# Two expert layers: the last quarter of the down-projection's columns from each token's own fetched rows

## What is computed

```
u = u_emb[expert]
a = jax.nn.gelu(jnp.einsum('thk,td->thk' ...), approximate=False)
coef = (g * a).astype(xb.dtype)
return jnp.einsum('thk,thkd->td', coef, v_emb[expert])
```

## Time and profile before

| | |
|---|---|
| median of 3 runs | 4169.73 us |
| profiled execution, span | 4171.1 us |
| TensorE, VectorE, ScalarE, GpSimd busy | 99%, 74%, 55%, 12% |
| DMA | 831 MB, 199 GB/s over the span |
| down-projection of block 1, of block 2 | 1457 to 2154 us, 3450 to 4147 us |

### The profile page before, as it was taken

How to read it: one execution, slowest core, us unless ns; L and a number is a source line. 1 busy time by engine, 2 the same in 40 slices (tenths; PEclk the granted TensorE clock), 3 DMA queues, 4 the chain that set the end, 5 groups by cost and what they waited for, 6 DMA issues and landing times.

```text
span 4171.1 us, 72720 instructions
## 1 busy us (share of the span) xinstructions
PE 4116.5 (99%) x21876; PEld 3527.9 (85%) x21876; DVE 3099.3 (74%) x5278; ACT 2278.5 (55%) x4043; POOL 516.1 (12%) x509
## 2 busy tenths in 40 slices
PE   8999999999999999999999999999999999999998
PEld 8978898888888888888889899988888888888887
DVE  6476677885999766777769978688599985566666
ACT  5446544555666655555554465455566665555554
POOL 4100010000222211111100002000022221111110
PEclk9999999999999999999999999999999999999999
...
GB/s 223 163 121 150 202 175 194 207 207 197 191 192 191 201 220 219 231 261 246 239 212 178 176 153 184 163 210 206 199 193 190 190 198 221 216 218 238 216 219 161
DMA packets 310247, 831.31 MB, mean 199 GB/s; under 512 B 29040, under 2 KB 129136, under 8 KB 306800
## 3 DMA queue, kind: packets, MB, share of 16 engines
...
...
HBM read 779.37 MB, written 50.33 MB: 199 GB/s over the span
## 4 chain that ended last, share of the span: by engine, by line
PE 94%; DVE 4%; ACT 1%; issue 1%; DMA 0%; DVEq 0%; SPq 0%; ACTq 0%
PE psum L419 11%; PE psum L417 11%; PE psum L418 11%; PE psum L485 11%; PE psum L487 11%; PE psum L486 11%; PE psum L1717 5%; PE psum L1719 5%; PE psum L1718 5%; PE psum L1909 2%; PE psum L1911 2%; PE psum L1910 2%; PE psum L408 1%; DVE sb_w_lo L2297 1%; PE psum L426 1%; PE psum L1815 1%
## 5 line engine op out<-in xcount | busy, mean ns | idle before, releaser
L2297 DVE TENSOR_TENSOR sb_w_lo<-sb_raw,sb_w_hi 128x512 fp32r<-128x512 f32 x2736 | 1887.1, 712 | 986.5 <-ACT sb_w_hi L1998 975.5
L1998 ACT CAST sb_w_hi<-sb_raw 128x512 fp32r<-128x512 f32 x2736 | 1696.9, 623 | 1581.2 <-PE psum L487 645.0
L417 PE MATMUL psum<-sb_w_hi,sb_act_hl 128*128 128x512 f32 x2048 | 811.4, 396 | 1.1 <-DVE sb_w_lo L2297 1.1
L419 PE MATMUL psum<-sb_w_lo,sb_act_hl 128*128 128x512 f32 x2048 | 801.5, 391 | 0.0
L418 PE MATMUL psum<-sb_w_hi,sb_act_hl 128*128 128x512 f32 x2048 | 798.9, 390 | 0.0
L485 PE MATMUL psum<-sb_w_hi,sb_act_hl 128*128 128x512 f32 x2048 | 797.0, 389 | 0.8 <-DVE sb_w_lo L2297 0.8
L486 PE MATMUL psum<-sb_w_lo,sb_act_hl 128*128 128x512 f32 x2048 | 796.7, 389 | 0.0
L487 PE MATMUL psum<-sb_w_hi,sb_act_hl 128*128 128x512 f32 x2048 | 796.7, 389 | 0.0
L1717 PE MATMUL psum<-sb_act_hl,sb_w_hi 128*128 128x256 f32 x1488 | 429.8, 289 | 26.9 <-DVE sb_w_lo L2297 13.8
L419 PEld LDWEIGHTS psum<-sb_w_lo,sb_act_hl 128*128 128x128 f32 x2048 | 385.0, 188 | 82.1
L485 PEld LDWEIGHTS psum<-sb_w_hi,sb_act_hl 128*128 128x128 f32 x2048 | 384.4, 188 | 81.0 <-DVE sb_w_lo L2297 1.2
...
## 6 DMA issues: line engine op xcount, KB each, us to landing
sb_raw<-in_u SPq DMA_DIRECT2D x512, 512.0 KB, 4.2
sb_raw<-in_v SPq DMA_DIRECT2D x512, 512.0 KB, 3.5
...
sb_acts_in<-acts_mid SPq DMA_DIRECT2D x256, 128.0 KB, 3.3
acts_mid<-sb_acts_out SPq DMA_DIRECT2D x126, 256.0 KB, 5.4
...
```

The source lines that it names most:

```text
L417: pe.matmul(ps, h, w_hi[:, c, :], start=k == 0, stop=False)
L419: return pe.matmul(ps, h, w_lo[:, c, :], start=False, stop=k == 15)
L1998: act.copy(w_hi[:, c, :], raw[:, 2 * par + c // 2, (c % 2) * 512:(c % 2) * 512 + 512]).then_inc(hi_ready, 1)
L2297: dve.tensor_tensor(w_lo[:, c, :], raw[:, 2 * par + c // 2, (c % 2) * 512:(c % 2) * 512 + 512], w_hi[:, c, :].bitcast(F32), ALU.subtract). ...
```

## The change

v is cut by columns. The first 1536 (DENSE) stay dense: three quarters a tile, 18 matmuls, loads of 128x1024 and 128x512, w_hi and w_lo used as a ring of four (`down_slot`). The last 512 (PICKED) come per token: GpSimd issues an indirect DMA that fetches the 2 KB pieces of a token's own 128 experts, one per partition, into picked_rows, and another that fetches its 128 activations, 4 bytes each, from acts_mid. Four tokens (t x 128 + 32j + r, j = 0 to 3) are a group ("quad"), 64 a block, four in flight (QUAD_SLOTS). VectorE (`place`) multiplies activation and gate, and writes the coefficients into column r of a zero 128x32 matrix per token (lone). TensorE (`quad`) multiplies it with the token's rows in plain fp32 into partitions 32j to 32j+31 of bank 6 + t. Two groups follow each other behind tiles 7, 11, 15 and so on to 123, 126 and 127. GpSimd's weighing moves to VectorE; GpSimd starts with the row fetches of four groups, then their activations, then group by group as quad_used rises. VectorE makes the indices ahead of tile 0 (`make_indices`). The tiles of TensorE and VectorE in these stages are written out instead of looped, the buffers of the fetched rows lie over act_hl and scratch, and some semaphores are merged.

The core of the diff:

```diff
+PICKED = 512
+DENSE = D - PICKED
+QUADS, QUAD_SLOTS = 64, 4
...
+def quad_tile(q):
+    return min(7 + 4 * (q // 2), 96 + q // 2, 127)
+QUADS_AFTER = [[q for q in range(QUADS) if quad_tile(q) == i] for i in range(128)]
...
+        picked = nc.alloc_sbuf_tensor_at("sb_picked", [P, 14, 512], F32, offset=act_at + 2 * 512 * 4).ap()
+        picked_rows = [picked[:, n, :] for n in range(14)]
+        picked_rows += [scratch[:, lo:lo + 2, :].rearrange("p a b -> p (a b)") for lo in (4, 6)]
+        lone = scratch[:, 0:2, :].rearrange("p a b -> p (a b)").rearrange("p (n j m) -> p n j m", n=QUAD_SLOTS, j=4)
+        picked_acts, one_of, picked_coef = scratch[:, 2, :], scratch[:, 3, 0:63], scratch[:, 3, 64:80].rearrange("p (n j) -> p n j", j=4)
+        v_index, act_index = slots[:, 1, :].bitcast(U32), slots[:, 2, :].bitcast(U32)
+        by_quad = lambda v: v.rearrange("p (t j r) -> p t r j", t=QT, j=4)
...
+        def down_slot(k, c):
+            return (3 * k + c) % 4
...
-            def out_tile(i, par, first):
+            def out_tile(i, k, first=False):
                 pe.wait_ge(c_lo, i + (128 * (blk - 1) + 1))
-                for c in range(4):
+                for c in range(3):
+                    n = down_slot(k, c)
                     if first and c == 1:
                         pe.wait_ge(acts_made, 64 * blk)
                     pe.wait_ge(lo_ready, (i + b) * 4 + c + 1)
                     for t in range(QT):
                         ps = psum[:, 2 * c + t, :]
-                        c_h, c_l = (act_hl[:, par, lo + t * P:lo + t * P + P] for lo in (0, T))
-                        pe.matmul(ps, c_h, w_hi[:, c, :], start=first, stop=False, skip_group_check=True)
-                        pe.matmul(ps, c_h, w_lo[:, c, :], start=False, stop=False, skip_group_check=True)
-                        mm = pe.matmul(ps, c_l, w_hi[:, c, :], start=False, stop=False, skip_group_check=True)
-                    mm.then_inc(quarter_used, 1)
-            out_tile(0, 0, True)
-            tiles(pe, 1, 128, lambda i, u: out_tile(i, (1 + u) % 2, False))
+                        c_h, c_l = (act_hl[:, k % 2, lo + t * P:lo + t * P + P] for lo in (0, T))
+                        pe.matmul(ps, c_h, w_hi[:, n, :], start=first, stop=False, skip_group_check=True)
+                        pe.matmul(ps, c_h, w_lo[:, n, :], start=False, stop=False, skip_group_check=True)
+                        mm = pe.matmul(ps, c_l, w_hi[:, n, :], start=False, stop=False, skip_group_check=True)
+                    mm.then_inc(quarter_used, 1 if c < 2 else 2)
+            def quad(q):
+                n, (t, r) = q % QUAD_SLOTS, divmod(q, 32)
+                pe.wait_ge(lone_ready, QUADS * (blk - 1) + q + 1)
+                for j in range(4):
+                    mm = pe.matmul(psum[32 * j:32 * j + 32, 6 + t, :], lone[:, n, j, :], picked_rows[4 * n + j],
+                                   start=r == 0, stop=False, skip_group_check=True)
+                mm.then_inc(quad_used, 1)
+            for i in range(128):
+                out_tile(i, i % 4, i == 0)
+                for q in QUADS_AFTER[i]:
+                    quad(q)
...
+            def split_down(i, k):
+                par = (b + k) % 2
+                for c in range(3):
+                    j = 2 * par + c // 2
+                    if c != 1:
+                        act.wait_ge(raw_loaded[j], (i + (b - par)) * 8 + 16)
+                    act.wait_ge(quarter_used, i * 4 + (4 * b + c - 4) + (isinstance(i, int) and i == 0))
+                    act.copy(w_hi[:, down_slot(k, c), :], raw[:, j, (c % 2) * 512:(c % 2) * 512 + 512]).then_inc(hi_ready, 1 if c < 2 else 2)
+            def high(i, k):
+                first = isinstance(i, int) and i == 0
+                if not first:
+                    act.wait_ge(quarter_used, i * 4 + (4 * b - 4))
+                act.wait_ge(weighed, i + (128 * (blk - 1) + 1))
+                act.copy(act_hl[:, k % 2, 0:T], gate_e[:, i, :]).then_inc(c_hi, 1)
+                split_down(i, k)
...
+                if c == 3:
+                    act.wait_ge(quad_used, QUADS * blk)
...
-            def lows(i, u):
+            def make_indices():
+                dve.wait_ge(hot_ready, h0 + GROUPS)
+                one, two = slots[:, 1, :], slots[:, 2, :]
+                dve.scalar_tensor_tensor(gate_parts[:, 0, :], one, float(NKEYS), two, ALU.mult, ALU.add)
+                link(dve.scalar_tensor_tensor(gate_parts[:, 1, :], two, float(NKEYS), one, ALU.mult, ALU.add))
+                link(dve.tensor_copy(v_index, gate_parts[:, 0, :]))
+                for t in range(QT):
+                    ins = dve.scalar_tensor_tensor(gate_parts[:, 0, t * P:t * P + P], gate_parts[:, 1, t * P:t * P + P], float(T), iota, ALU.mult, ALU.add)
+                link(ins)
+                dve.tensor_copy(act_index[:, 0:P], gate_parts[:, 0, 0:P])
+                dve.tensor_scalar(act_index[:, P:T], gate_parts[:, 0, P:T], float(P), None, ALU.add).then_inc(index_made, 1)
+                dve.memset(one_of, 0.0).then_inc(index_made, 1)
+                dve.wait_ge(index_made, 3 * blk - 1)
+                dve.memset(one_of[:, 31:32], 1.0).then_inc(index_made, 1)
+                dve.wait_ge(index_made, 3 * blk)
...
+            def weigh(i):
+                dve.wait_ge(acts_loaded[i % 2], (i - i % 2) * 8 + (16 + 1024 * (blk - 1)))
+                e = gate_e[:, i, :]
+                dve.tensor_tensor(e, acts_in[:, i % 2, :], e, ALU.mult).then_inc(weighed, 1)
+            def place(q):
+                n, (t, r) = q % QUAD_SLOTS, divmod(q, 32)
+                dve.wait_ge(picked_loaded[n], 128 * (QUADS // QUAD_SLOTS * (blk - 1) + q // QUAD_SLOTS + 1))
+                if q >= QUAD_SLOTS:
+                    dve.wait_ge(quad_used, QUADS * (blk - 1) + q - QUAD_SLOTS + 1)
+                link(dve.tensor_tensor(picked_coef[:, n, :], by_quad(picked_acts)[:, t, r, :], by_quad(slots[:, 0, :])[:, t, r, :], ALU.mult))
+                wide = [P, 4, 32]
+                dve.tensor_tensor(lone[:, n], picked_coef[:, n, :].unsqueeze(2).broadcast_to(wide),
+                                  one_of[:, 31 - r:63 - r].unsqueeze(1).broadcast_to(wide), ALU.mult).then_inc(lone_ready, 1)
+            def lows(i):
+                if i < 127:
+                    weigh(i + 1)
                 dve.wait_ge(c_hi, i + (128 * (blk - 1) + 1))
-                dve.tensor_tensor(act_hl[:, u, T:2 * T], gate_e[:, i, :], act_hl[:, u, 0:T].bitcast(F32), ALU.subtract).then_inc(c_lo, 1)
-                low(i + b, (b + u) % 2)
+                dve.tensor_tensor(act_hl[:, i % 2, T:2 * T], gate_e[:, i, :], act_hl[:, i % 2, 0:T].bitcast(F32), ALU.subtract).then_inc(c_lo, 1)
+                par = (b + i) % 2
+                for c in range(3):
+                    n = down_slot(i, c)
+                    dve.wait_ge(hi_ready, (i + b) * 4 + (c + 1))
+                    dve.tensor_tensor(w_lo[:, n, :], raw[:, 2 * par + c // 2, (c % 2) * 512:(c % 2) * 512 + 512],
+                                      w_hi[:, n, :].bitcast(F32), ALU.subtract).then_inc(lo_ready, 1 if c < 2 else 2)
+                for q in QUADS_AFTER[i]:
+                    place(q)
...
+                down, v = base[f"v{blk}"], a[f"v{blk}"]
+                def load_down(i, k):
+                    for h, n in enumerate((1024, 512)):
+                        slot = 2 * ((down + k) % 2) + h
+                        sp.wait_ge(lo_ready, i * 4 + (4 * down + 2 * h - 6))
+                        sp.dma_start(raw[:, slot, 0:n], v[i, :, 1024 * h:1024 * h + n]).then_inc(raw_loaded[slot], 16)
+                def tile_down(i, k):
+                    acts_back(blk, i + 1, (k + 1) % 2, True)
+                    load_down(i, k)
...
-                stream(f"v{blk}", a[f"v{blk}"], between={64: lambda: residual_back(blk), 110: all_stored, 127: lambda: None}, beside=fetch, apart=3)
+                load_down(0, 0)
+                load_down(1, 1)
+                sp.wait_ge(rows_turned, 2 * UP_GROUPS * blk + 6)
+                for j in range(2):
+                    acts_back(blk, j, j, blk == 2)
+                acts_leave(blk, UP_GROUPS - 1, 0, acts_four)
+                acts_leave(blk, UP_GROUPS - 1, 1, last_acts[:, 2, :].rearrange("p (n c) -> p n c", n=4))
+                acts_back(blk, 2, 0, True)
+                fours(sp, 2, 64, tile_down)
+                residual_back(blk)
+                fours(sp, 64, 110, tile_down)
+                all_stored()
+                fours(sp, 110, 127, tile_down)
+                load_down(127, 3)
...
-                def weigh(i, slot):
-                    pool.wait_ge(acts_loaded[slot], (i - slot) * 8 + (16 + 1024 * blk))
-                    e = gate_e[:, i, :]
-                    pool.tensor_tensor(e, acts_in[:, slot, :], e, ALU.mult).then_inc(weighed, 1)
-                tiles(pool, 0, 128, weigh)
+                v_rows, acts_flat = a[f"picked_v{blk + 1}"], acts_mid.rearrange("n p (t o) -> (n p t) o", o=1)
```

(44 more changed lines are left out.)

77 lines of the change are left out of this document (31 added, 46 removed).

## The result

The changed kernel takes 4539.8 us in the median of 4 runs (4527.5 to 4552.7), the kernel before 4170.4 beside it (4169.3 to 4171.8): ratio 1.088, 95% interval 1.086 to 1.091. It is 9% slower, 546 us above the forecast and far outside its range. The profiled execution spans 4525.7 us.

A forecast was written before the change was run, and what follows sets the result against it. TensorE was taken to bound the down-projection stages by matmul count times cadence. 4171.1 - 348.2 + 137.6 + 5 + 30 = 3995.5, less 1.4 for profile against median: 3994 us; likeliest case 3935 to 4040, whole range up to 4220.

The forecast's parts named there:

- What goes: Dense down-projection tiles on TensorE: 18 matmuls instead of 24 in 256 tiles, -348.2 us, all on the path.
- what TensorE gets: Matmuls of the fetched groups: 64 pairs of groups at 2.15 us, +137.6 us.
- the round: Four tiles and a pair take TensorE 18.5 us instead of 21.8; VectorE, ScalarE and v loads were to fit.
- the sum without fetches: Both stages without delays from fetches: 4171 - 348 + 138 + 5, about 3966 us.
- GpSimd's price: Cost of one indirect DMA on GpSimd: hidden under 1.15 us, stage longer than before above 1.36; taken as hidden.
- rival 1: GpSimd's issues set the pace, from 1.36 us each on; at 1.5 us each 4330 us, slower; chance 0.23.
- a loss not counted: A granted TensorE clock under full in the down-projection stages, named without a size.
- My marks for "right": Signs of success: TensorE always busy, tiles every 4.08 us, GpSimd waiting for quad_used between bursts, place without waits.
- Rival 2: DMA engines, or GpSimd at 1.15 to 1.36 us an issue, set the pace; near 4057 us, still faster; chance 0.28.
- the late loads: Loads landing late at times because the DMA engines are near full: half a microsecond a pair, +30 us.
- Rival 3: The four matmuls of a group do not overlap on TensorE: 459 us instead of 137.6, 4316 us; chance 0.02.
- The start: Start of each stage, with index ops and 16 row fetches beside the first v loads: 2.5 us a block, +5.

The follow-up runs named there:

- e1: Changed kernel with only the first four groups fetched in a block (32 of 512 indirect DMAs), all groups still multiplied: 4020.0 us, ratio 0.964.
- e5: Changed kernel with row fetches behind the first four groups replaced by a second fetch of the 4-byte values, still 16 a round: 4495.8 us, ratio 1.078.
- e6: Changed kernel, but GpSimd waits after each group's 8 indirect DMAs until they have landed: 4451.8 us, ratio 1.067.
- e12: Changed kernel with fetched rows for 128 of 256 tokens, GpSimd waiting for each four indirect DMAs to land: 4106.5 us, ratio 0.985.
- e15: Changed kernel with one small GpSimd product (128x128, into unused columns) behind each four indirect DMAs: 4351.3 us, ratio 1.045.
- e2: Changed kernel without the 4-byte value fetches behind the first four groups, row fetches kept: 4047.9 us, ratio 0.971.
- e7: e1, but GpSimd waits after each four of a block's first 32 indirect DMAs until they have landed: 4003.6 us, ratio 0.960.

## Why the prediction was wrong

- **What goes, what TensorE gets, the round**: right. 18.44 us for 18.5 (e1); the sum without fetches is met within some 5 us once the first fetches' 53 us are in it. (The lower end of my range, 4171 - 348 + 110, is 3933 and not 3935; nothing hangs on it.)
- **GpSimd's price, the step that failed first.** I took it as hidden, "near the lower end" (0.33 us), because what is to be done is an issue. It is 0.94 us, and 0.30 until the next: 1.25 at best, 21.0/16 = 1.31 in the mean, for 2 KB rows and 4-byte values alike. That is above the 1.15 up to which I had called it hidden, and just under 1.36, from which rival 1 began. The Trainium skill, DMA: Bandwidth & Descriptors, Specifications, puts the first byte of a DMA issued by GpSimd at about 1 us. No run here shows that latency; taken as the cost of an issue, it is near the 0.94 but leaves out the 0.30 gap, and so gave 16 us a round. By GpSimd's time alone the kernel would be at 4020 + 62 x 2.5 = 4175 us, no change.
- **The other 365 us no case had: the second step that failed.** Rival 1 has the engine and the sign, not the mechanism: its mark, VectorE waiting for fetches, is absent. I counted GpSimd's issues as its own time only, and never as something that could hold up TensorE's signals. Those are late in long unbroken rows of indirect DMAs (337 of 610, and e5, e6, e12, e15), and half clock follows the gaps, which I had named as a loss not counted: a clock of 0.87 to 0.88 in the stages, and 172 us more in which TensorE is busy.
- **My marks for "right" misled.** "GpSimd waiting for quad_used between bursts of 16; VectorE's place without waits" is just what the slow kernel shows. They tell that GpSimd's rate is not the bound, not that its work is harmless.
- **Rival 2 and the late loads**: the DMA half falls. The share is 0.65 to 0.68 in the stages, and with the rows alone (e2) 302 GB/s at 0.88 to 0.90 cost TensorE a few per cent. ScalarE waits 28 us for v loads in the changed kernel; my +30 us was of the right size and beside the point.
- **Rival 3**: a group is about as forecast; e1's round leaves 18.44 - 72 x 0.2267 = 2.1 us for a pair, where I had 2.15.
- **The start**: 53 us in both blocks together, not 5, from 32 fetches in a row. Pauses (e7) take the late signals away and put a wait for the first groups in their place, so only 16 us are gained.
